# Latent queries and keys made feature-major, their rotary rows placed by transfers, and compressed attention taken into the middle of those products

## The chip, the cores and the metric

The kernel runs on one core of one Trainium2 chip. The metric is the device time of one execution in microseconds (us). The engines are named as in the profile: PE is TensorE (its matmuls), PEld its weight loads, DVE is VectorE, ACT is ScalarE, POOL is GpSimd, SP is SyncE, which here only issues transfers. Everything is in float32; a kernel before took 1770.38 us, the median of three runs (1769.51 to 1771.64).

## The reference

Two transformer blocks over 512 tokens and 1024 features: the first mixes native sparse attention (compressed, selected and windowed) with multi-head latent attention and ends in a gated convolutional feed-forward; the second has a Hyena and Fourier mixer and a mixture of 32 experts. The change touches the part of the first block between its input projection and its attention loop:

```python
proj = h @ w_in[i]
q_n, kv_n, gate_n, c_q, c_kv, k_r, merge = jnp.split(proj, offsets, axis=-1)
# compressed keys and values: 31 blocks of 32 tokens, stride 16
kb = (k[:, blk] + pos).reshape(B, n_cmp, G, CMP_BLOCK * dh)
k_cmp = jax.nn.gelu(kb @ w1 + b1) @ w2                      # and v_cmp alike
s_c = einsum('btgrd,bjgd->bgrtj', q, k_cmp) * scale - slopes * dist_c
p_cmp = _masked_softmax(s_c, dist_c >= 0);  o_cmp = p_cmp @ v_cmp
# latent attention: 8 heads, 64 plain + 32 rotary features in q and k, 64 in v
q  = (_rmsnorm(c_q, g_q) @ w_uq).reshape(B, T, H, QK_NOPE + QK_ROPE)
q_rope = _rope(q[..., QK_NOPE:], cos, sin)
kv = (_rmsnorm(c_kv, g_kv) @ w_ukv).reshape(B, T, H, QK_NOPE + V_DIM)
k_r = _rope(k_rope, cos, sin)                               # one set of rotary keys for all heads
s = (q_nope @ k_nope + q_rope @ k_r) * scale
```

## The kernel before, in words

Each engine has one hand-written program; semaphores order them. Weights come as 128x1024 tiles (`W[n]`) through a ring of 12 slots: SP waits until `w_used` says that tile n - 12 was used, then issues the load of tile n (L1469). PSUM is one array `pb` of eight banks of 128x512. A name such as `arena` in the profile is one large SBUF tensor which holds most of what is named below (`qTm`, `kTm`, `Vm`, `cqkv`, `chat`, `qkt`, `Pc`); `junk` is a separate 128x1024 scratch.

The stage in question starts when PE ends the products of the value columns and gates (L365, `split_columns`). After it PE does, in order:

1. the compression of keys and values, 256 small matmuls of 64x31 (L1661), ACT's GELUs (L1895, L1899), the second layer (L1669, L1670);
2. twelve transposes of the normed latents `chat` (L1677), copied by ACT into `cqT` (L1903);
3. four rounds, one for each 128 tokens: the up-projections of queries (L1691) and of keys and values (L1694), token-major; ACT copies the queries and DVE the keys and values into `qkt` (L1912, L2155 to L2157), DVE turns the rotary part (L2164 to L2169), PE transposes all 16 head tiles of queries and keys back to feature-major (L1705), and DVE and ACT copy them into `qTm` and `kTm` (L2172, L1916). `qkt` has two halves, but a round's transposes wait for its own copies, and the next round's products wait for the PSUM banks of this one;
4. compressed attention: scores of all heads against 31 blocks (L1716), a softmax of DVE and ACT over `Pc` (L2178 to L2202, ACT's exponential L1921), eight transposes (L1786), and the products with the compressed values (L1792). `scores(0)`, the first scores of the loop (L1740), stand before the transposes.

Then the attention loop runs: 48 units of two heads, in 12 groups `(i, kind)` of query tile and branch. Kind 2 is latent attention, its first unit is unit 16. `combine(w)` multiplies a finished group by its spread inverse sums; for the selected and windowed branches it writes into `junk` (L2240), first at unit 8. GpSimd (`h_back`, L1490) rebuilds `hT` from its two parts right after the value products; the DVE and ACT rounds wait for the end of it, because `qkt` overlays what it reads. After the loop come merge, output projection, feed-forward and the second block, whose last part, the experts, streams its weights.

SP sits in a loop over ring slots (L1469); the program raises `w_used` by 3 for the up-projection weights inside the compressed scores (L1716).

## Time and profile before

| | us |
|---|---|
| median of three runs (lowest, highest) | 1770.38 (1769.51, 1771.64) |
| the profiled execution, its own time | 1771.91 |
| its span from first to last instruction | 1770.1 |
| mean granted TensorE clock, 1 is 2.4 GHz | 0.939 |
| PE busy over the span | 1517.0 (86%) |
| DVE, ACT, POOL busy | 598.8, 477.2, 493.1 |

The profiled execution lasted 1.8 us longer than its span. Busy shares are means over stages with very different limits: the dense products of the first block, the attention loop, and the expert stream. For this change the table of the stretch from 95 to 180 us is what matters, since the work before and behind it is the same in both kernels. PEclk is the clock that was granted to TensorE: 1.00 is 2.4 GHz, 0.50 is 1.2 GHz.

### The profile page before, as it was taken

The numbers are of one execution on the slowest core, as the hardware profiler recorded it, in microseconds if no ns is written. First come the engines' busy times: TensorE is split into PE (matmuls) and PEld (weight loads), VectorE is DVE, ScalarE is ACT, GpSimd is POOL, SyncE is SP. The second block draws the span as 40 slices with busy tenths as digits, with TensorE's granted clock in tenths as the row PEclk, the third lists the DMA queues.
The fourth block names the chain that finished last, engine by engine and source line by source line (L and its number), as shares of the span: only waits on it lengthen the run. The fifth ranks groups of instructions, "written<-read, shape, count | busy, mean of one in ns | idle before, by whom it ended". The sixth has DMA issues, their size and how long they took to land.

```text
span 1770.1 us, 18813 instructions
## 1 busy us (share of the span) xinstructions
PE 1517.0 (86%) x7192; PEld 997.3 (56%) x7193; DVE 598.8 (34%) x1010; ACT 477.2 (27%) x818; POOL 493.1 (28%) x298
## 2 busy tenths in 40 slices
PE   7986999999979999999996999895877787877871
PEld 5964556788758888878774765474332232322320
DVE  3244565322263333322327685746100000000003
ACT  4232566322243333321325334221100000000001
POOL 3430113444334444444422362521101010000001
PEclk9986999999989999999997999996899999999996
DMA  7320000233223323323222221154699999999983
GB/s 277 103 84 36 1 1 2 84 95 96 83 83 96 95 96 95 96 89 92 93 84 89 84 71 60 48 209 183 274 426 427 427 428 425 426 422 425 425 343 150
DMA packets 47045, 315.25 MB, mean 178 GB/s; under 512 B 7344, under 2 KB 7344, under 8 KB 34560
## 3 DMA queue, kind: packets, MB, share of 16 engines
q1 hardware_dynamic: 37296, 286.80, 42.2%
q0 software_dynamic: 9104, 25.40, 3.9%
q10 hardware_dynamic: 576, 2.10, 0.3%
q8 instruction: 47, 0.77, 0.2%
q14 instruction: 22, 0.18, 0.0%
HBM read 307.98 MB, written 14.68 MB: 182 GB/s over the span
## 4 chain that ended last, share of the span: by engine, by line
PE 63%; DMA 19%; DVE 11%; issue 3%; ACT 2%; POOL 1%; SPq 0%; POOLq 0%; DVEq 0%; ACTq 0%
PE banks L355 23%; DMA arena<-experts 18%; PE banks L385 11%; PE banks L922 8%; PE banks L1821 2%; PE banks L365 2%; PE banks L1753 2%; PE banks L833 2%; PE banks L1769 1%; PE banks L690 1%; PE banks L1736 1%; PE banks L691 1%; PE banks L1740 1%; DVE arena_r L1611 1%; PE banks L1691 1%
## 5 line engine op out<-in xcount | busy, mean ns | idle before, releaser
L333 POOL TENSOR_TENSOR arena_r<-ring,arena_r 128x1024 fp32r<-128x1024 f32 x143 | 353.5, 2473 | 512.5 <-ACT arena_r L318 512.5
L355 PE MATMUL banks<-hT_r,arena_r 128*128 128x512 f32 x1216 | 397.0, 396 | 8.4 <-DVE arena_r L1611 5.7
L922 PE MATMUL banks<-ring,arena 128*64 128x512 f32 x768 | 245.4, 625 | 62.7 <-DMA arena<-experts 43.2
L355 PE MATMUL banks<-arena_r 128*128 128x512 f32 x800 | 295.8, 394 | 0.0
L318 ACT ACTIVATE arena_r<-ring 128x1024 fp32r<-128x1024 f32 x143 | 151.2, 1058 | 524.5 <-PE banks L355 325.0
L355 PEld LDWEIGHTS banks<-hT_r,arena_r 128*128 128x128 f32 x1216 | 228.4, 188 | 72.1 <-issue 8.9
L922 PEld LDWEIGHTS banks<-ring,arena 128*64 128x64 f32 x768 | 80.4, 144 | 215.5 <-issue 160.0
L385 PE MATMUL banks<-arena_r 128*128 128x512 f32 x784 | 187.9, 394 | 3.6 <-POOL arena_r L333 3.6
L355 PEld LDWEIGHTS banks<-arena_r 128*128 128x128 f32 x800 | 150.2, 188 | 35.0
L385 PEld LDWEIGHTS banks<-arena_r 128*128 128x128 f32 x784 | 147.2, 188 | 38.6 <-POOL arena_r L333 5.3
L589 POOL DMA_INDIRECT back<-arena,at_out x16 | 16.3, 1020 | 442.0 <-DVE arena L1386 228.9
L944 PE MATMUL banks<-arena 128*64 128x512 f32 x512 | 120.2, 624 | 21.3 <-DMA arena<-experts 15.8
L922 PE MATMUL banks<-arena 128*64 128x512 f32 x256 | 129.9, 666 | 0.0
L1381 DVE TENSOR_TENSOR arena<-arena,banks 128x512 f32<-128x512 f32 x16 | 11.0, 688 | 297.1 <-PE banks L922 297.1
L944 PEld LDWEIGHTS banks<-arena 128*64 128x64 f32 x512 | 40.9, 142 | 90.3 <-issue 78.7
L2320 DVE SCALAR_TENSOR_TENSOR arena<-banks,colt,arena 128x511 f32<-128x511 f32 x44 | 33.0, 749 | 157.5 <-ACT arena L2011 157.5
L1386 DVE COPY arena<-banks 128x512 f32<-128x512 f32 x16 | 11.1, 692 | 154.2 <-PE banks L944 154.2
L1589 PE MATMUL banks<-cst,arena 128*128 128x128 f32 x160 | 28.1, 349 | 39.0 <-DVE arena L1563 26.3
L1073 ACT ACTIVATE arena<-banks 128x512 f32<-128x512 f32 x16 | 9.6, 597 | 186.5 <-PE banks L930 186.5
L1934 ACT ACTIVATE arena<-banks,st 128x512 f32<-128x512 f32 (+3 forms) x96 | 49.9, 528 | 22.5 <-DVE st L2215 21.9
L344 DVE CAST arena_r<-arena 128x512 fp32r<-128x512 f32 x30 | 14.1, 471 | 111.7 <-PE banks L385 111.7
L1589 PEld LDWEIGHTS banks<-cst,arena 128*128 128x128 f32 x160 | 25.1, 184 | 42.5 <-issue 20.1
(404 smaller groups left out, 1882.8 us busy)
## 6 DMA issues: line engine op xcount, KB each, us to landing
arena<-experts SPq DMA_DIRECT2D x48, 2048.0 KB, 21.2
ring<-experts SPq DMA_DIRECT2D x48, 2048.0 KB, 18.2
ring<-stream SPq DMA_DIRECT2D x163, 512.0 KB, 3.5
rows<-arena POOLq DMA_DIRECT2D x8, 512.0 KB, 6.2
arena<-back POOLq DMA_DIRECT2D x8, 512.0 KB, 7.3
grow<-grows POOLq DMA_DIRECT2D x5, 512.0 KB, 4.6
resid<-x ACTq DMA_DIRECT2D x4, 512.0 KB, 5.5
out<-arena POOLq DMA_DIRECT2D x4, 512.0 KB, 3.0
```

The source lines that it names most:

```text
L318: nc.scalar.activation(parts(name, m)[:, 0, :], tile(tile_n), ACT.Copy).then_inc(S["w_high"], 1)
L333: nc.gpsimd.tensor_tensor(w[:, 1, :], tile(tile_n), plain(w[:, 0, :]), ALU.subtract).then_inc(S["w_low"], 1)
L355: last = nc.tensor.matmul(pb[:, bank, :], w[:, a, k * P:(k + 1) * P], b[:, k, :], start=(k == 0 and part == 0), stop=(k == ND - 1 and part ...
L365: last = nc.tensor.matmul(pb[:, bank0 + i, 0:width], a[:, k, i * P:(i + 1) * P], w[:, v, q * width:(q + 1) * width], start=(k == 0 and par ...
L385: last = nc.tensor.matmul(pb[:, 2 * i + h, :], u[row], w[:, v, h * 512:(h + 1) * 512], start=(k == 0 and part == 0), stop=(k == K - 1 and ...
L833: last = nc.tensor.matmul(pb[:, 2 * i + h, :], rows[row][:, i * P:(i + 1) * P], w[:, v, h * 512:(h + 1) * 512], start=(k == 0 and part == ...
L922: last = nc.tensor.matmul(pb[r, bank, :], XT[:, k, r], chunk(c + e)[:, k * 512:(k + 1) * 512], start=(k == 0), stop=(k == ND - 1))
L944: last = nc.tensor.matmul(pb[r, 3 + h, :], hbT[:, k, r], chunk(4 + e)[:, k * D + h * 512:k * D + (h + 1) * 512], start=(k == 0), stop=(k = ...
L1589: ins = nc.tensor.transpose(pb[:, bank0 + b, a * P:(a + 1) * P], src[:, a, b * P:(b + 1) * P], ident)
L1753: last = nc.tensor.transpose(pb[:, 4 + hh, kt * P:(kt + 1) * P], Pr[:, u % 2, hh, kt * P:(kt + 1) * P], ident)
L1821: last = nc.tensor.matmul(pb[:, b + w, :], tw[:, u, (4 * w + k) * P:(4 * w + k + 1) * P], src[:, k, :], start=(k == 0 and part == 0), stop ...
L1934: nc.scalar.activation(Pr[:, u % 2, hh, 0:nk], pb[:, 2 * (u % 2) + hh, 0:nk], ACT.Exp, scale=-1.0, bias=nm[:, u % 2, hh:hh + 1], accum_out ...
```

## The change

- The 64 transposes, and the token-major `qkt`, are gone. The weights are laid out anew on the host, so that the stationary operand is a weight block and the moving one is `cqT` with its 512 tokens: each product gives 128 features by 512 tokens, which is already the form of `qTm` and `kTm`. Two products hold the first and second rotary halves of the queries of all heads; four hold the plain query parts of heads j and j+4 (`q_nope`), four the plain keys of such pairs, and four, token-major still, the values.
- Cosine and sine, spread over the heads in `wide`, and the rotated keys (written back into `cqkv`) are transposed by PE (8 and 4 transposes), the first two scaled on the way (`cosT`, `sinT`). DVE multiplies both query halves with both (4 products of 128x512), GpSimd takes their difference and sum into `q_first` and `q_second`, the two halves of `junk`.
- Transfers within SBUF, issued by SP, put things in their places: one moves the plain queries of heads 4 to 7 from partitions 64 to 127 down to 0 to 63, one the keys likewise; 16 small ones place the rotary query rows by head; two copy the rotary keys for heads 5 to 7 and 0 to 3. SP issues them in its program order, behind the ring load of tile 33 and ahead of tile 34.
- The order on PE is new: transposes of the latents first, then compression, then the first three query products, the second layer of compression, a query product, the compressed scores, and behind them the ten remaining products, while DVE and ACT do the softmax of compressed attention. Its exponential stands on ACT behind three of the four copies of values.
- ACT's sine and square root come before its wait for the value products, and the gates are copied raw and put through the sigmoid later.
- New waits: each latent score waits for all 18 transfers (`qk_in`), and so does `combine(0)`; the first copies of turned probabilities wait for GpSimd's two (`q_rope`).

The diff, cut to what the prediction speaks of (the other hunks change PSUM bank numbers, semaphore names, the host's weight layout and 12 unused constant columns):

```diff
--- before.py
+++ after.py
...
-        qkt = ar(21216, 3072).rearrange("p (u w c) -> p u w c", u=2, w=2)
+        wide = ar3(23264, 2, 512)
+        cosT, sinT = ar(20192, 512), ar(20704, 512)
+        q_first, q_second = junk[:, 0:512], junk[:, 512:1024]
+        crossed = [ar(23264, 512), ar(23776, 512)]
...
-            with sp.Fori(1, W_EXP // RING) as turn:
+            def load(n):
+                sp.wait_ge(S["w_used"], n + 1 - RING)
+                sp.dma_start(ring[:, n % RING, :], W[n, :, :]).then_inc(landed[n % RING], 16)
+
+            def q_rows(h):
+                for part, src in enumerate((q_first, q_second)):
+                    at = DH + 16 * part
+                    sp.dma_start(qTm[at:at + 16, h, :], src[16 * h:16 * h + 16, :]).then_inc(S["qk_in"], 16)
+
+            def k_rows(a, b):
+                sp.dma_start(kTm[DH:QK, a:b, :], kTm[DH:QK, 4:5, :].broadcast_to([32, b - a, T])).then_inc(S["qk_in"], 16)
+
+            for n in range(RING, W_MERGE + RING):
+                load(n)
+
+            sp.wait_ge(S["mla_act"], 5)
+            sp.dma_start(qTm[0:DH, 4:8, :], qTm[DH:P, 0:4, :]).then_inc(S["shift_in"], 16)
+            k_rows(5, 8)
+            sp.wait_ge(S["q_rope"], 2)
+            for h in range(4, 8):
+                q_rows(h)
+            sp.wait_ge(S["shift_in"], 16)
+            for h in range(4):
+                q_rows(h)
+            sp.wait_ge(S["mla_act"], 11)
+            sp.wait_ge(S["mla_dve"], 11)
+            sp.dma_start(kTm[0:DH, 4:8, :], kTm[DH:P, 0:4, :]).then_inc(S["shift_in"], 16)
+            sp.wait_ge(S["shift_in"], 32)
+            k_rows(0, 4)
+            for n in range(W_MERGE + RING, 3 * RING):
+                load(n)
...
+            pool.wait_ge(S["mla_dve"], 9)
+            nc.gpsimd.tensor_tensor(q_first, q_first, crossed[0], ALU.subtract).then_inc(S["q_rope"], 1)
+            nc.gpsimd.tensor_tensor(q_second, q_second, crossed[1], ALU.add).then_inc(S["q_rope"], 1)
...
+            pe.wait_ge(S["mla_norm"], 1)
+            for b in range(3):
+                for i in range(NT):
+                    last = nc.tensor.transpose(pb[:, b, i * P:(i + 1) * P], chat[:, i, b * P:(b + 1) * P], ident)
+                last.then_inc(S["mla_tr"], 1)
+
+            pe.wait_ge(S["proj_v_ev"], 2)
+            for b, bank in ((0, 3), (1, 6)):
+                pe.wait_ge(S["mla_dve"], b + 1)
+                for i in range(NT):
+                    last = nc.tensor.transpose(pb[:, bank, i * P:(i + 1) * P], wide[:, b, i * P:(i + 1) * P], ident)
+                last.then_inc(S["mla_tr"], 1)
+            pe.wait_ge(S["mla_dve"], 3)
+            for i in range(NT):
+                last = nc.tensor.transpose(pb[0:QK, 7, i * P:(i + 1) * P], cqkv[:, i, 320:416], ident)
+            last.then_inc(S["mla_tr"], 1)
+
             pe.wait_ge(S["cmp_blocks"], 4)
-            pe.wait_ge(S["proj_mla_ev"], NT)
...
+            for n in (W_UQ, W_UQ + 1, W_UKV):
+                arrived(pe, n)
+
+            def q_up(at, bank):
+                for k in range(2):
+                    last = nc.tensor.matmul(pb[:, bank, :], tile(W_UQ + k)[:, at:at + P], cqT[:, k, :], start=(k == 0), stop=(k == 1))
+                return last
+
+            def q_nope(j, bank):
+                q_up(256 + j * P, bank).then_inc(S["mla_up"], 1)
+
+            pe.wait_ge(S["mla_tr_ev"], 3)
+            q_up(0, 0)
+            q_up(P, 1).then_inc(S["mla_up"], 1)
+            q_nope(0, 2)
...
             pe.wait_ge(S["cmp_gelu"], 5)
+            pe.wait_ge(S["mla_dve"], 5)
...
+            q_nope(1, 3)
...
+            q_nope(2, 4)
+            pe.wait_ge(S["mla_dve"], 9)
+            q_nope(3, 0)
+
+            for i, bank in enumerate((7, 1, 2, 3)):
+                pe.wait_ge(S["mla_act"], (1, 1, 2, 3)[i])
+                nc.tensor.matmul(pb[:, bank, :], cqT[:, 2, i * P:(i + 1) * P], tile(W_UKV)[:, 512:1024], start=True, stop=True)\
+                    .then_inc(S["mla_up"], 1)
+            for j, bank in enumerate((6, 5, 4, 7)):
+                if j == 0:
+                    pe.wait_ge(S["cs_dve"], 1)
+                if j >= 2:
+                    pe.wait_ge(S["mla_act"], (4, 6)[j - 2])
+                last = nc.tensor.matmul(pb[:, bank, :], tile(W_UKV)[:, j * P:(j + 1) * P], cqT[:, 2, :], start=True, stop=True)
+                last.then_inc(*((S["mla_up"], 1) if j < 3 else (used, 3)))
...
+            pe.wait_ge(S["mla_act"], 7)
...
+            nc.scalar.activation(gates[:, :, :], pb[:, 4:8, 256:280], ACT.Copy).then_inc(S["proj_v_ev"], 1)
+            nc.scalar.activation(Vsw[:, :, :], pb[:, 4:8, 0:256], ACT.Copy).then_inc(S["proj_v_ev"], 1)
+            for b in range(3):
+                act.wait_ge(S["mla_tr"], b + 1)
+                nc.scalar.activation(cqT[:, b, :], pb[:, b, :], ACT.Copy,
+                                     scale=col("g_q", b) if b < 2 else col("g_kv")).then_inc(S["mla_tr_ev"], 1)
+            act.wait_ge(S["proj_v_ev"], 1)
+            nc.scalar.activation(gates[:, :, :], gates[:, :, :], ACT.Sigmoid).then_inc(S["proj_v_ev"], 1)
...
+            act.wait_ge(S["mla_tr"], 6)
+            nc.scalar.activation(kTm[DH:QK, 4, :], pb[DH:QK, 7, :], ACT.Copy).then_inc(S["mla_act"], 1)
+            for j, bank in enumerate((2, 3, 4, 0)):
+                act.wait_ge(S["mla_up"], 2 + j)
+                nc.scalar.activation(qTm[:, j, :], pb[:, bank, :], ACT.Copy, scale=QK_SCALE).then_inc(S["mla_act"], 1)
+
+            def v_up(i):
+                act.wait_ge(S["mla_up"], 6 + i)
+                nc.scalar.activation(Vm[:, i, :], pb[:, (7, 1, 2, 3)[i], :], ACT.Copy).then_inc(S["mla_act"], 1)
+
+            for i in range(3):
+                v_up(i)
             act.wait_ge(S["cs_dve"], 2)
             nc.scalar.activation(Pc[:, :, :, 0:31], Pc[:, :, :, 0:31], ACT.Exp).then_inc(S["cs_act"], 1)
+            v_up(3)
+            for j, bank in enumerate((6, 5)):
+                act.wait_ge(S["mla_up"], 10 + j)
+                nc.scalar.activation(kTm[:, j, :], pb[:, bank, :], ACT.Copy).then_inc(S["mla_act"], 1)
...
+            for b, t in enumerate((cos, sin)):
+                nc.vector.tensor_copy(wide[:, b, :].rearrange("p (i h f) -> p i h f", i=NT, h=HEADS),
+                                      by_tile(t).unsqueeze(2).broadcast_to([P, NT, HEADS, 16])).then_inc(S["mla_dve"], 1)
...
+            nc.vector.tensor_tensor(by_tile(r1), x1, by_tile(cos), ALU.mult)
+            nc.vector.tensor_tensor(by_tile(r2), x2, by_tile(sin), ALU.mult)
+            nc.vector.tensor_tensor(by_tile(r3), x2, by_tile(cos), ALU.mult)
+            L(nc.vector.tensor_tensor(by_tile(r4), x1, by_tile(sin), ALU.mult))
+            nc.vector.tensor_tensor(x1, by_tile(r1), by_tile(r2), ALU.subtract)
+            nc.vector.tensor_tensor(x2, by_tile(r3), by_tile(r4), ALU.add).then_inc(S["mla_dve"], 1)
+
+            for b, (dst, bank) in enumerate(((cosT, 3), (sinT, 6))):
+                dve.wait_ge(S["mla_tr"], 4 + b)
+                nc.vector.tensor_scalar(dst, pb[:, bank, :], QK_SCALE, None, ALU.mult).then_inc(S["mla_dve"], 1)
+
+            dve.wait_ge(S["mla_up"], 1)
+            dve.wait_ge(S["mla_dve"], 5)
+            for dst, bank, t in ((q_first, 0, cosT), (crossed[1], 0, sinT), (q_second, 1, cosT), (crossed[0], 1, sinT)):
+                nc.vector.tensor_tensor(dst, pb[:, bank, :], t, ALU.mult).then_inc(S["mla_dve"], 1)
...
+                    if w == 0:
+                        dve.wait_ge(S["qk_in"], 16 * 18)
...
+            dve.wait_ge(S["h_back"], ND)
+            for j, bank in ((2, 4), (3, 7)):
+                dve.wait_ge(*((S["mla_up"], 12) if j == 2 else (S["w_used"], W_MERGE)))
+                nc.vector.tensor_copy(kTm[:, j, :], pb[:, bank, :]).then_inc(S["mla_dve"], 1)
```

In both kernels a float32 matmul is one row here and two instructions in the trace. PE behind the value products, before (`cst` is the identity of a transpose, `ring` a weight tile, 64x31 the compression):

```order
L365 MATMUL banks<-arena_r 128x280
L1661 MATMUL banks<-arena,ring 64x31 [waits w_landed3,proj_mla_ev,cmp_blocks]
L1661 MATMUL banks<-arena,ring 64x31 x31
...
L1669 MATMUL banks<-arena,colt 64x31 [waits cmp_gelu]
L1670 MATMUL banks<-colt,arena 128x64
...
L1677 MATMUL banks<-cst,arena 128x128 [waits mla_norm,proj_v_ev]
L1677 MATMUL banks<-cst,arena 128x128 x11
```

and in the changed kernel:

```order
L1693 MATMUL banks<-cst,arena 128x128 [waits mla_norm]
L1693 MATMUL banks<-cst,arena 128x128 x11
L1700 MATMUL banks<-cst,arena 128x128 [waits mla_dve,proj_v_ev]
...
L1704 MATMUL banks<-cst,arena 96x128 [waits mla_dve]
L1704 MATMUL banks<-cst,arena 96x128 x3
L1714 MATMUL banks<-arena,ring 64x31 [waits w_landed3,cmp_blocks]
L1714 MATMUL banks<-arena,ring 64x31 x31
```

The transposes of the latents moved ahead of compression, and 12 more joined them; compression now waits for nothing of the latents but stands behind them.

PE from the second layer of compression on, before (96x128 are transposes of head tiles, 128x31 the compressed scores that follow later):

```order
L1677 MATMUL banks<-cst,arena 128x128 [waits mla_norm,proj_v_ev]
L1677 MATMUL banks<-cst,arena 128x128 x11
L1691 MATMUL banks<-ring,arena 128x384 [waits w_landed8,w_landed7,w_landed9,cmp_ready,mla_tr_ev]
L1691 MATMUL banks<-ring,arena 128x384 x3
L1694 MATMUL banks<-ring,arena 128x512 x2
L1705 MATMUL banks<-cst,arena 96x128 [waits kv_ev,q_ev]
L1705 MATMUL banks<-cst,arena 96x128 x15
L1691 MATMUL banks<-ring,arena 128x384 [waits kv_ev,q_ev]
```

and in the changed kernel (128x512 with `ring` are the up-projections, 128x31 the compressed scores):

```order
L1724 MATMUL banks<-arena,ring 128x512 [waits w_landed9,mla_tr_ev,w_landed8,w_landed7]
L1724 MATMUL banks<-arena,ring 128x512 x5
L1739 MATMUL banks<-arena,colt 64x31 [waits mla_dve,cmp_gelu]
L1740 MATMUL banks<-colt,arena 128x64
L1739 MATMUL banks<-arena,colt 64x31
L1740 MATMUL banks<-colt,arena 128x64
L1724 MATMUL banks<-arena,ring 128x512 x2
L1750 MATMUL banks<-arena 128x31 [waits cmp_ready]
L1750 MATMUL banks<-arena 128x31 x31
L1724 MATMUL banks<-arena,ring 128x512 x2
L1724 MATMUL banks<-arena,ring 128x512 [waits mla_dve]
L1724 MATMUL banks<-arena,ring 128x512
```

The rounds of product and transposes became one row of products, with the compressed scores after the fifth group of them; nothing that waits for a copy of a whole round is left.

ACT behind the GELUs in the changed kernel (32x512 the rotary keys, then four query copies, value copies, the exponential, key copies); before, four rounds of one 128x768 and two 96x4x128 copies stood there, and the exponential behind them all:

```order
L1960 ACTIVATE arena<-banks 32x512 [waits mla_tr,h_back]
L1963 ACTIVATE arena<-banks 128x512 [waits mla_up] x4
L1967 ACTIVATE arena<-banks 128x512 [waits mla_up] x3
L1972 ACT_TABLE_LOAD
L1972 ACTIVATE arena<-arena 128x32x31 [waits cs_dve]
L1967 ACTIVATE arena<-banks 128x512 [waits mla_up]
L1976 ACTIVATE arena<-banks 128x512 [waits mla_up] x2
L1979 ACTIVATE arena<-banks 128x512 [waits cs_pe] x2
```

The exponential of compressed attention now stands between the third and the fourth copy of values, so it can't begin before the third value product.

SP in the changed kernel from the ring loads on (64x2048 the moves of heads 4 to 7, 16x512 the rotary query rows, 32x3x512 and 32x4x512 the rotary keys):

```order
L1470 DMA ring<-stream 128x1024 [waits w_used] x22
L1484 DMA arena<-arena 64x2048 [waits mla_act]
L1478 DMA arena<-arena 32x3x512
L1475 DMA arena<-junk 16x512 [waits q_rope]
L1475 DMA arena<-junk 16x512 x7
L1475 DMA arena<-junk 16x512 [waits shift_in]
L1475 DMA arena<-junk 16x512 x7
L1494 DMA arena<-arena 64x2048 [waits mla_dve,mla_act]
L1478 DMA arena<-arena 32x4x512 [waits shift_in]
L1470 DMA ring<-stream 128x1024 [waits w_used] x2
```

All 20 transfers stand behind the last of the 22 ring loads, which waits for the last up-projection; before there was nothing between the ring loads.

## Rows read from the trace of the kernel before

**Rows 1.** Windows: stretch, length, busy us of PE, PEld, DVE, ACT, POOL; clock, DMA share, GB/s.
```profile
95.00:180.00 85.00, 61.02 (x482) 40.90 (x481) 36.02 (x78) 24.11 (x38) 11.86 (x10) 0.74 0.16 50
```
**Rows 2.** The chain that ended last, 109 to 180 us: start, length, what.
```profile
109.56 5.10 PE banks L1691 x8
...
124.00 1.73 PE banks L1694 x4
125.97 0.68 DVE arena L2156
...
171.08 1.98 PE banks L1786 x8
...
179.99 0.42 PE banks L1740 x4
```
**Rows 3.** Groups of instructions, 90 to 185 us: busy, mean ns, idle before.
```profile
L1705 PE MATMUL banks<-cst,arena 128*96 128x128 f32 x64 | 12.2, 368 | 11.8 <-DVE arena L2169 11.8
...
L1661 PE MATMUL banks<-arena,ring 64*64 64x31 f32 x256 | 7.8, 218 | 0.2 <-issue 0.2
...
L1716 PE MATMUL banks<-arena 64*128 64x31 f32 x64 | 4.6, 304 | 0.7 <-ACT arena L1916 0.7
```
**Rows 4.** Timeline of DVE, ACT and POOL, 90 to 107 us: start, length, instruction.
```profile
90.72 0.15 DVE L2113 TENSOR_SCALAR st<-st 128x4 f32<-128x4 f32 x1
94.98 1.02 ACT L1886 ACTIVATE arena<-banks 128x1024 f32<-128x1024 f32 x1 [6.66 <-PE banks L365]
95.02 11.26 POOL L1490 TENSOR_TENSOR hT<-hT_r,arena_r 128x512 f32<-128x512 f32 x8 [4.24 <-PE banks L365]
99.21 1.28 ACT L1892 ACT_TABLE_LOAD   x1
100.98 1.29 DVE L2116 TENSOR_TENSOR arena<-arena,st 128x1024 f32<-128x1024 f32 x1
103.86 1.28 DVE L2129 TENSOR_TENSOR arena<-arena 128x64 f32<-128x64 f32 x1
106.40 0.22 DVE L2131 TENSOR_TENSOR arena<-arena 128x64 f32<-128x64 f32 x1
```
**Rows 5.** Timeline of PE: three kinds of float32 products at half clock.
```profile
105.02 0.68 PE L1670 MATMUL banks<-colt,arena 64*128 64x64 f32 x2
105.63 2.82 PE L1677 MATMUL banks<-cst,arena 128*128 128x128 f32 x12
173.73 6.26 PE L1792 MATMUL banks<-arena 128*64 128x512 f32 x16 [0.69 <-ACT arena L1924]
```
**Rows 6.** Windows of 2 us; columns as in rows 1.
```profile
104.00:106.00 2.00, 2.00 (x10) 1.64 (x9) 1.97 (x2) 0.00 (x0) 2.00 (x2) 0.50 0.68 256
114.00:116.00 2.00, 2.00 (x6) 0.76 (x4) 0.00 (x0) 0.00 (x0) 0.00 (x0) 0.96 0.00 0
124.00:126.00 2.00, 1.72 (x5) 0.41 (x3) 0.24 (x2) 0.24 (x1) 0.00 (x0) 1.00 0.00 0
160.00:162.00 2.00, 0.41 (x4) 0.27 (x4) 1.21 (x2) 0.00 (x0) 0.00 (x0) 0.50 1.03 420
```
**Rows 7.** Timeline: steps of the softmax, and copies.
```profile
107.61 1.84 DVE L2140 COPY arena<-banks 32x64 f32<-32x64 f32 x8
116.48 0.29 DVE L2155 COPY arena<-arena 128x256 f32<-128x256 f32 x1 [7.03 <-PE banks L1694]
161.71 1.26 DVE L2181 TENSOR_TENSOR arena<-banks,arena 128x496 f32<-128x496 f32 x2
166.67 1.03 ACT L1921 ACTIVATE arena<-arena 128x992 f32<-128x992 f32 x1 [9.61 <-DVE arena L2191]
199.13 0.69 DVE L2240 TENSOR_TENSOR junk<-banks,arena 128x512 f32<-128x512 f32 x1 [1.03 <-ACT arena L1949]
```
**Rows 8.** SP's three ring loads at 157 us: shortest, median, longest issue in ns, and landing.
```profile
L1469 SPq DMA_DIRECT2D ring<-stream x3: 332/333/1453, 157.1 to 158.3; - x3
...
DMA to landing us min/median/max: 4.6/5.3/5.9
```

148 lines of the change are left out of this document (34 added, 114 removed).

## The prediction, made before the changed kernel had run

> **What bounds the kernel now.** I read the page first, then windows, the chain, the groups by line and the timeline of the stretch from 95 to 180 us. The change touches only this stretch; what stands before and behind it is the same work in the same order. There PE is busy 61.0 of 85.0 us, at a mean clock of 0.74, and DVE, ACT and POOL are each busy under half of it [rows 1]: no engine is full, so the stage is a chain of hand-overs. The chain shows them: products at 109.56, then in the second round products until 125.7, DVE from 125.97, and so on until the loop starts at 179.99 [rows 2]. The transposes of the four rounds hold PE for 12.2 us and it stands 11.8 us before them, waiting for DVE [rows 3]. Then the compressed scores (4.6 us) and a softmax beside which PE does nearly nothing: the first addition at 161.71, the exponential at 166.67, the transposes at 171.08, then 6.26 us of products at half clock [rows 2, 5, 7].
>
> **The stretch anew, step by step.** I rebuild it from 94.9 us, the end of the value products, to the first unit of the loop, and take the difference to the 180.0 of now. Moments are estimates from the rows' durations, with 0.25 us from PE to a reader and 0.05 between others, my own allowance.
>
> *Prices.* A float32 product of 128x512 over 128 rows is two instructions; four take 1.73 us on the chain at 124.00 [rows 2], where the clock is 1.00 [rows 6]: 0.43 each, 0.86 a product, double at half clock. A transpose is 2.82/12 = 0.23 at half clock [rows 5], about 0.11 at full. A copy or product of DVE or ACT out of PSUM with 512 columns is 0.69 [rows 7].
>
> *Norm and rotary tables.* ACT's sine and root now come in the 6.66 us in which it waited for the value products [rows 4], each behind a table load of 1.28. The row sums are ready at 90.87 [rows 4]. DVE then does two new spread copies (0.29 for 256 columns [rows 7], so 0.56 each), 0.2, 1.29 and half of 1.29: the normed latents are there at about 94.1, before PE wants them. So the norm, now awaited from 100.98 on, is off the path.
>
> *Transposes ahead of compression.* 12 + 8 + 4 of them, 24 x 0.11 = 2.6 us. The last four want the rotated keys, six small steps of DVE. Four fit before 95.0; the last two fall beside POOL's eight additions, where a step of 64 columns took 1.28 against 0.22 after they ended [rows 4]. So keys at 97.8, compression from 98.1: 3.2 us later than now. (Without that contention 97.5, so the price has both ends within 0.6.)
>
> *Compression*: 7.8 us [rows 3] at full clock. Now the clock reads 0.50 from 104 on [rows 6], some 9 us after the dense products ended. I let it fall at the same moment: compression ends at 107.9, 2.0 us of that from the clock.
>
> *First three query products*: 6 x 0.86 = 5.2 us. Now the clock is back to 0.96 in 114 to 116 [rows 6], 4.5 us after dense products began at 109.56. The same here gives half clock to 112.4 and adds 2.2: 115.3. ACT's GELUs (1.1 us after compression) lie beside them.
>
> *Second layer and ready*: four small products, 1.0 us (two took 0.68 at half clock [rows 5]): 116.3. Then DVE's nine copies, 0.2 + 1.84 [rows 7], and a hand-over at each end: 118.7. One query group (two products, 1.7) lies beside them. DVE's four products with the tables (2.8 us) start at 114 and end just as these copies may start. POOL's two additions (11.26/8 = 1.4 us each [rows 4]) now fall beside the nine copies, which read PSUM; no row shows such a pair. Nothing is one end; if both block the copies, as they do a step within SBUF, 2.8 us is the other. I take nothing, since PSUM steps don't look like those of L2129, and keep 2.8 for the range.
>
> The Trainium skill, "SBUF — State Buffer", section "SBUF: two separate sides", says that GpSimd shuts out a DVE step only where that has two SBUF inputs or runs in a two-port mode. [...]
>
> *Compressed scores*: 4.6 us for 64 instructions now, of which the last part ran at half clock, since 160 to 162 reads 0.50 [rows 3, 6]. I take 4.2: 123.0. This was at 160.4.
>
> *The other products*: two query groups (four products), four of values, four of keys, 12 x 0.86 = 10.3, and 1.5 for a clock that falls in the small scores once more and comes back at 126: 134.8. In all there are 20 such products for 24 of before with as many columns (20 x 512 = 16 x 384 + 8 x 512), so nothing is saved in them. Saved are 64 transposes and the hand-overs around them.
>
> *The softmax beside them.* From the first addition to the exponential it is 161.71 to 166.67 [rows 7], 5.0 us, so DVE's part is done at 128.3. But the exponential stands behind three value copies on ACT: the third value product ends after 7 x 0.86 + 1.5, at 130.5, its copy at 131.4, the table load (1.28 [rows 4]) at 132.7, the exponential (1.03 [rows 7]) at 133.7. From its end to the transposes DVE now takes 167.70 to 171.08 [rows 2, 7], 3.4 us: 137.1. Here ACT's order ends last, and DVE has 3 us to spare.
>
> *Transposes and products with compressed values*: 8 x 0.11, ACT's second copy 0.7, 3.3 us for what took 6.26 at half clock [rows 5], hand-overs 0.5: the loop starts at 142.5 if the clock is full, as dense products ran until 134.8.
>
> So 180.0 - 142.5 = 37.5 us earlier.
>
> **What could give it back in the loop.** The 20 transfers stand on SP behind the load of tile 33, which waits for the last key product, 134.8. Three ring loads go first and land 4.6 to 5.9 us after their issue [rows 8]. Of the transfers no row of this kernel shows the like (within SBUF, half the partitions, 512 KB for the two largest). Lower bound: the issues alone, 20 x 0.33 = 7 us [rows 8]. Upper: four steps that wait for one another (ring loads, query move, key move, key rows), 5.9 us each, and the issues: 134.8 + 23.6 + 7 = 165. I take 5.3 for the loads and 4 for each later step, half the issues hidden: 154. The first who waits is `combine(0)`, now at 199.13, 19.1 us after the loop starts [rows 7]: at 161.6. So there are 7 us of cover by my value, and 4 us are lost at the upper bound. The first latent score is unit 16, later still. POOL's two additions end by 120, and who waits for them starts behind 140.
>
> Trainium skill, "SBUF — State Buffer", section "Door 1: The DMA port swizzle": partitions 0 to 63 reach only half of the ports, so a 64-row transfer gets no more bandwidth than a 32-row one, 196 GB/s for 1 MiB. By that page the two moves of 512 KB are an estimated 2.7 us of transfer more than a fixed 2 us each, which would leave the sum as it is; no row shows it yet.
>
> **Sum.** The profiled execution took 1771.91; less 37.5 gives 1734.4. The median of three lies 1.5 below that execution, so the forecast for the median is **1733**.
>
> **Rivals.**
> 1. *The clock stays halved.* For: the compression and the compressed scores are small products, and the stretch now runs at 0.74, at 0.50 in its softmax [rows 1, 6]. Against: dense products brought it back within 5 us. If it is 0.50 from 104 to the end of the stage, the rebuild gives compressed scores at 130.6, keys at 150.9, loop at 162.5: 17.5 saved, 1753. If it halves only from the compressed scores on, 154.5, and 1745.
> 2. *The transfers come late*, at the upper bound or somewhat beyond: 4 to 12 us lost, 1737 to 1745. For: 18 of them on one semaphore, and each step waits for the one before. Against: 27 us between the last product and the wait.
> 3. *Full clock throughout*: small products keep the clock up when they stand in a dense stream. Then the loop starts at 136: 1727. Against: PE was busy all of 104 to 106, with 0.50 [rows 6]. The Trainium skill, "TensorE: Matmul & The Clock Gate", section "What's actually happening", says that a busy array releases the throttle and idleness brings it back; by that the clock would hold here, as in this rival.
> 4. *Slower than before.* One mechanism: the transfers within SBUF run on one of the 16 engines each instead of on all. 420 GB/s [rows 6] is 26 GB/s per engine. Two moves of 512 KB are then 20 us each, 448 KB of rotary keys 17, 16 rows of 32 KB another 20: 77 us behind 140 ends at 217, and `combine(0)`, which needs them at 161.6, waits 55. That is 18 us slower, 1788. It decides from 59 us of transfers on: 21.6 of cover behind 140, and the 37.5 gained. Against: the ring loads, of the same kind of issue, use all engines.
> 5. *The change does not do what it says*, for instance something outside the rebuilt stretch holds the loop, and the time stays within 0.2%: nothing in the chain speaks for it.
>
> **Chances.** Forecast (1729 to 1741) 0.63; rival 1 0.14; rival 2 0.09; rival 3 0.08; rival 4 0.04; rival 5 0.02. All but the last two are faster. What a measurement of this kernel can tell from no change is about 0.2%, 3.5 us. Faster 0.94, same 0.02, slower 0.04. The range is 1726 to 1752: it holds the forecast, rivals 2 and 3 and most of rival 1.
>
> **What will show it.** In the changed trace: compression (now L1714) starting at 98 and not 95; PE's products in one run with the compressed scores at 119 to 123; the exponential waiting for the copy of values (its predecessor on ACT) and not for DVE; compressed values' transposes at 137; the first score of unit 1 at 142; the granted clock 1.00 from 126 on. `combine(0)` should wait for ACT's spread inverse as now and for no DMA. The forecast is wrong if the clock reads 0.50 behind 126, if DVE idles before L2204 or PE before the compressed scores by more than 2 us, or if the span from loop start to the end is not what it is now, 1590 us.

## The result, and the profile after

| | before | after |
|---|---|---|
| median, us (lowest, highest) | 1770.44 (1769.51, 1771.64) | 1727.51 (1726.66, 1730.80) |
| profiled execution; its span | 1771.91; 1770.1 | 1730.80; 1729.0 |
| mean granted clock | 0.939 | 0.948 |
| PE busy; DVE, ACT, POOL busy | 1517.0; 598.8, 477.2, 493.1 | 1497.3; 586.5, 475.4, 494.1 |

The ratio is 0.9761 (95% interval 0.9744 to 0.9778): 42.9 us faster. Forecast were 1733, with a range of 1726 to 1752. The measured time lies in the range, but 1.5 us below the forecast's own band of 1729 to 1741, which had a chance of 0.63.

The windows of the rebuilt stretch in the changed kernel, from the end of the value products to the first score of the loop, and four windows of 2 us in it (columns as in rows 1):

```profile
94.09:137.12 43.03, 41.16 (x427) 25.21 (x426) 18.10 (x34) 19.02 (x34) 12.93 (x12) 0.96 0.34 108
114.00:116.00 2.00, 2.00 (x40) 2.00 (x40) 0.33 (x1) 0.00 (x0) 0.00 (x0) 1.00 0.04 8
116.00:118.00 2.00, 2.00 (x20) 1.45 (x19) 0.93 (x2) 0.00 (x0) 0.00 (x0) 0.75 0.00 0
118.00:120.00 2.00, 2.00 (x4) 0.85 (x3) 1.93 (x3) 0.00 (x0) 0.00 (x0) 0.50 0.00 0
120.00:122.00 2.00, 2.00 (x5) 0.76 (x4) 1.97 (x2) 0.60 (x1) 0.00 (x0) 0.90 0.00 0
```

Read it against [rows 1]: 43.0 us for 85.0. PE stood idle for 24.0 us then (85.00 - 61.02) and for 1.9 now (43.03 - 41.16), 22.1 less; and it was busy 19.9 us less, at a clock of 0.96 for 0.74. The last four rows show the one place where the clock still falls, in the compressed scores.

The chain that ended last, in the changed kernel (start, length, what; L1693 transposes of the latents, L1714 compression, L1724 queries, L1750 compressed scores, L1759 values, L1834 turned probabilities, L1842 products with compressed values):

```profile
94.25 1.31 PE banks L1693 x12
...
97.04 7.58 PE banks L1714 x256
104.62 5.35 PE banks L1724 x12
...
113.20 3.76 PE banks L1750 x64
116.96 5.33 PE banks L1724 x8
122.28 2.59 PE banks L1759 x6
124.89 0.60 ACT arena L1967
...
126.81 1.04 ACT arena L1972
127.87 1.20 DVE st L2229
...
131.22 0.67 PE banks L1834 x4
...
133.05 3.65 PE banks L1842 x16
...
137.12 1.02 PE banks L1800 x8
```

Where [rows 2] change engine in every round, this is PE's own work from 94 to 125, with one stretch of DVE (the copies at 111.2 to 113.2, beside a query group), then one passage through ACT and DVE. The loop starts at 137.12; [rows 2] had it at 179.99. That is 42.9 us earlier: 42.2 of them lie in the stretch (from the end of the value products, 94.94 before and 94.25 now, it is 85.05 us before and 42.87 now), and 0.7 lie ahead of it, in work that the change doesn't touch.

The timeline of the changed kernel, the instructions that the prediction named (L2192 the last step of the rotated keys, L2207 the copies answering to L2140 of [rows 7], L1527 the first of two additions, the second follows at 112.08, L2278 `combine(0)`):

```profile
93.62 0.22 DVE L2192 TENSOR_TENSOR arena<-arena 128x64 f32<-128x64 f32 x1
94.33 9.85 POOL L1524 TENSOR_TENSOR hT<-hT_r,arena_r 128x512 f32<-128x512 f32 x8 [4.20 <-PE banks L368]
110.86 1.26 POOL L1527 TENSOR_TENSOR junk<-junk,arena 128x512 f32<-128x512 f32 x1 [6.67 <-DVE arena L2201]
111.30 1.84 DVE L2207 COPY arena<-banks 32x64 f32<-32x64 f32 x8
...
127.87 1.19 DVE L2229 TENSOR_REDUCE st<-arena 128x32 f32<-128x992 f32 x1 [5.87 <-ACT arena L1972]
155.82 0.69 DVE L2278 TENSOR_TENSOR junk<-banks,arena 128x512 f32<-128x512 f32 x1 [1.01 <-issue]
```

DVE has done its part of the softmax at 122.0 (127.87 - 5.87) and then waits for ACT's exponential. `combine(0)` comes 18.7 us after the loop's start (19.1 before [rows 7]) and waits for no DMA.

SP's issues in the changed kernel (start, length of the group; L1484 and L1494 the moves of 512 KB, L1478 the rotary keys, L1475 the 16 query rows):

```profile
130.50 0.57 SPq L1484 DMA_DIRECT2D arena<-arena  x1
...
131.88 13.78 SPq L1475 DMA_DIRECT2D arena<-junk  x16
145.77 0.52 SPq L1494 DMA_DIRECT2D arena<-arena  x1
149.95 0.64 SPq L1478 DMA_DIRECT2D arena<-arena  x1
```

and the page's list of DMA issues for 100 to 200 us (name, count, KB each, median us to landing):

```profile
arena<-arena SPq DMA_DIRECT2D x2, 512.0 KB, 6.8
arena<-junk SPq DMA_DIRECT2D x16, 32.0 KB, 3.2
...
arena<-arena SPq DMA_DIRECT2D x1, 256.0 KB, 3.2
```

The last transfer lands at 149.95 + 3.2 = 153.2, 2.6 us before `combine(0)`. The 16 rows took 13.78 us to issue, 0.86 each. The two moves of 512 KB landed after 9.5 us (queries, behind three ring loads) and 4.2 us (keys).

### The profile page after: what moved, and what is told of

The parts are those of the page before. It is cut to its first block, busy times and chain, and to the rows that moved or that the text cites. A ratio compares the mean times of both kernels' runs of the same rounds, so it can differ in the third digit from the quotient of the medians.

```text
span 1729.0 us, 18608 instructions
## 1 busy us (share of the span) xinstructions
PE 1497.3 (87%) x7132; PEld 983.7 (57%) x7133; DVE 586.5 (34%) x976; ACT 475.4 (27%) x818; POOL 494.1 (29%) x300
## 4 chain that ended last, share of the span: by engine, by line
PE 64%; DMA 19%; DVE 10%; issue 3%; ACT 2%; POOL 1%; SPq 0%; POOLq 0%; ACTq 0%; DVEq 0%
PE banks L358 24%; DMA arena<-experts 18%; PE banks L388 11%; PE banks L925 9%; PE banks L1871 3%; PE banks L368 2%; PE banks L1800 2%; PE banks L836 2%; PE banks L1816 1%; PE banks L693 1%; PE banks L1783 1%; PE banks L694 1%; PE banks L1787 1%; DVE arena_r L1648 1%; PE banks L1626 1%
## 5 line engine op out<-in xcount | busy, mean ns | idle before, releaser
L388 PEld LDWEIGHTS banks<-arena_r 128*128 128x128 f32 x784 | 147.0, 188 | 39.5 <-POOL arena_r L336 5.3
L1626 PE MATMUL banks<-cst,arena 128*128 128x128 f32 x160 | 28.4, 353 | 39.5 <-DVE arena L1600 27.0
L347 DVE CAST arena_r<-arena 128x512 fp32r<-128x512 f32 x30 | 14.2, 472 | 112.1 <-PE banks L388 112.1
```

The costliest lines, as they stand in the source:

```text
L388: last = nc.tensor.matmul(pb[:, 2 * i + h, :], u[row], w[:, v, h * 512:(h + 1) * 512], start=(k == 0 and part == 0), stop=(k == K - 1 and ...
L1626: ins = nc.tensor.transpose(pb[:, bank0 + b, a * P:(a + 1) * P], src[:, a, b * P:(b + 1) * P], ident)
```

## The experiments

All are edits of the changed kernel, but for one of the kernel before. Ratios are to the kernel before, with 95% intervals; differences are of medians, and medians of the changed kernel itself, timed twice, differed by 0.9 us. A difference between two edits of under about 2 us is therefore read from the traces too, or called open. In comparisons a moment is counted from the end of the value products, since that wanders by a microsecond from profile to profile of the changed kernel and its edits (93.3 to 94.7).

**Compressed scores last.** They stand behind all products, and the softmax with them.

```diff
-            (64 compressed scores, behind q_nope(1, 3))
...
+            pe.wait_ge(S["mla_act"], 11)
+            (64 compressed scores, behind the key products)
```

> The changed kernel with its compressed scores moved behind all up-projections, and the exponential behind all value and key copies; everything else is kept. My theory: of the 43 us gained, a part comes from laying the softmax beside the ten remaining products. Without that, PE ends the products about 3.8 us earlier (at 124.8), does the scores until about 129.5 after ACT's last key copy, and then stands through DVE's 5.0 us, the exponential 1.0 and DVE's 3.4; transposes at about 139.5 instead of 131.2, and a falling clock adds up to 4 us in the products with compressed values: loop at 145 to 149 instead of 137.1, time 1736 to 1740. Rival: the softmax was never the last thing, only the feature-major form counts; then within 2 us of 1727.5.

Measured: 1735.81 us (1734.46 to 1736.93), ratio 0.9808 (0.9793 to 0.9823). PE's timeline at the turned probabilities in that kernel:

```profile
135.98 1.97 PE L1833 MATMUL banks<-cst,arena 128*128 128x128 f32 x8 [8.55 <-DVE arena L2234]
```

and two windows in the softmax:

```profile
126.00:128.00 2.00, 1.43 (x14) 0.60 (x12) 1.35 (x3) 0.00 (x0) 0.00 (x0) 1.00 0.95 238
...
134.00:136.00 2.00, 0.02 (x1) 0.02 (x1) 1.90 (x5) 0.00 (x0) 0.00 (x0) 0.50 0.29 66
```

PE waits 8.55 us for the softmax, in which the clock goes from 1.00 to 0.50, and the eight transposes behind it take 1.97 us for 1.09 in the version with all three edits (below). Taking the scores to the middle is worth 8.3 us, a fifth of the gain; by subtraction the other 34.6 come with the form and order of the products. From the end of the value products to the loop it is 51.2 us here for 42.9 in the changed kernel, the same 8.3.

**The norm early, alone**, in the kernel before: ACT's sine and square root ahead of its wait for the value products.

```diff
+            act.wait_ge(S["ang_ready"], 1)
+            nc.scalar.activation(ropet[:, 0:128], ropet[:, 128:256], ACT.Sin).then_inc(S["sin_ready"], 1)
+            act.wait_ge(S["mla_ms"], 1)
+            nc.scalar.activation(mrt, mss, ACT.Sqrt).then_inc(S["mla_rt"], 1)
             act.wait_ge(S["w_used"], W_CMP)
```

> The kernel before with one part of the change alone: ACT's sine and square root ahead of its wait for the value products. My theory: the norm was not on the path there, since PE does the compression (until 102.9) and its second layer first; the transposes could start about 0.0 to 0.5 us earlier, and DVE's small steps leave POOL's additions: 1769.5 to 1770.5. Rival: the norm and the rotary steps held up the copies that end cmp_ready, then 1 to 3 us are gained.

Measured: 1770.42 us (1769.26 to 1774.47), ratio 1.0003 (0.9993 to 1.0012). Nothing: in the old order compression and the second layer stand ahead of the latents' transposes, which start at 105.63 without a wait [rows 5]. The norm was not what ended last.

**The transposes' work, and their hand-overs.** Two kernels put 64 transposes back that nobody reads: the first in one run, the second in four lots that each wait for a copy.

```diff
+            pe.wait_ge(S["mla_act"], 1)
+            for n in range(64):
+                nc.tensor.transpose(pb[0:QK, 7, (n % 4) * P:(n % 4 + 1) * P], cqT[:, 2, 0:QK], ident)
             for i, bank in enumerate((7, 1, 2, 3)):
```
```diff
                     .then_inc(S["mla_up"], 1)
+                pe.wait_ge(S["mla_act"], 6 + i)
+                for n in range(16):
+                    nc.tensor.transpose(pb[0:QK, bank, (n % 4) * P:(n % 4 + 1) * P], cqT[:, 2, 0:QK], ident)
```

> The changed kernel, with 64 transposes of 96x128 added on TensorE in one run ahead of the first value product; they read the ready latents, write a bank that the product then overwrites, and nobody waits for them. It prices the work of the 64 transposes that the change took out, without their hand-overs. Theory A (work only): 64 x 0.13 us (what twelve took in the changed kernel, 1.5 us) = 8.3 us, all on the path, since the softmax's first part ends at 122 and the exponential stands behind the third value product: 1735.8 (1734.5 to 1737). Theory B (the clock is the real price of transposes: in the kernel before they took 12.2 us for 64): the granted clock falls to 0.50 within the run, 12 us for them and 3 or more for the products behind: 1742 or more. Theory C: they cost under 4 us, since the softmax covers them: 1731 or less.

> The same 64 transposes, but 16 behind each of the four value products, each lot waiting until ScalarE has copied that product, as the lots of the kernel before waited for their copies. The difference to the kernel with all 64 in one run is the price of four hand-overs in their shortest form (product, copy, transposes). Theory A: each hand-over leaves TensorE idle for one copy, 0.6 us, and 0.25 us on either side, 1.1 us; the fourth copy stands behind the exponential, table load and all, 1.3 + 1.0 us more: 3 x 1.1 + 3.5 = 6.8 us over the other kernel, 1742 to 1744. Rival: the waits also bring the clock down to 0.50, as in the kernel before: then another 5 us or more, 1747 or above.

Measured: 1734.63 us (1733.20 to 1736.94), ratio 0.9799 (0.9782 to 0.9815); and 1737.35 us (1736.45 to 1737.92), 0.9812 (0.9796 to 0.9828). The chain of the first has all 64 on it; in the chain of the second each lot has a hand-over of 0.02 + 0.61 + 0.04 us ahead of it. The chain of the first:

```profile
122.58 6.99 PE banks L1759 x64
```

and the second:

```profile
126.28 0.02 issue
126.31 0.61 ACT arena L1970
126.91 0.04 issue
126.96 1.95 PE banks L1763 x16
```

The work costs 7.1 us (7.0 on the chain, 0.109 each), four hand-overs in their shortest form 2.7 (4 x 0.67). I had set 0.13 for a transpose, from a group's busy time, and 6.8 us for the hand-overs: both too high, since the copy starts 0.02 us behind the product and the exponential fits between two lots. The clock read 1.00 in both from the first of these transposes to the last. So of the 42.9 us the transposes' work and their shortest hand-overs are 9.8. The kernel before lost more by the length of its waits (four rounds in which PE idled 3.0 us each, 11.8 in all [rows 3], where the shortest form costs 0.67), by the softmax, and by the clock. A token-major kernel with its rounds interleaved, which would keep the transposes and shorten the waits, was not run.

**The second layer early**: straight behind compression, where PE must wait for the GELUs.

```diff
+            (second layer, with its waits for cmp_gelu and mla_dve)
             pe.wait_ge(S["mla_tr_ev"], 3)
             q_up(0, 0)
```

> The changed kernel with the second layer of compression placed right behind the first, as in the kernel before, so that PE waits for ACT's GELUs and does small products before the first query products. Theory A, on the clock: it stayed at full because dense products followed the compression at once; with the wait of about 1 us and 1.2 us of small products it falls to 0.50 at about 105 as before, for some 4 us: 1.1 for the wait and 2 for the clock less about 1 for a compressed softmax that may start earlier, time 1729 to 1731. Theory B: the clock does not depend on this, only on what went before compression; then the clock stays at 1.00 until 117 and the time is 1727.5 to 1729.

Measured: 1731.77 us (1731.25 to 1735.70), ratio 0.9789 (0.9774 to 0.9804), 4.3 slower. PE's timeline in that kernel:

```profile
105.96 0.27 PE L1734 MATMUL banks<-arena,colt 64*64 64x31 f32 x2 [1.12 <-ACT arena L1955]
...
107.11 5.40 PE L1724 MATMUL banks<-arena,ring 128*128 128x512 f32 x8
```

and two windows:

```profile
106.00:108.00 2.00, 2.00 (x10) 1.39 (x11) 0.00 (x0) 0.32 (x1) 0.00 (x0) 0.96 0.88 277
108.00:110.00 2.00, 2.00 (x3) 0.67 (x2) 0.00 (x0) 0.00 (x0) 0.00 (x0) 0.50 0.23 92
```

A gap of 1.12 us and four small products, and the clock falls in the dense products behind them. In the kernel before it falls behind a wait for the same GELUs too, of 0.91 us, and there already in the small products (the 0.50 of [rows 6]):

```profile
103.80 0.33 PE L1669 MATMUL banks<-arena,colt 64*64 64x31 f32 x2 [0.91 <-ACT arena L1899]
```

By the profiles the loop starts 3.5 us later (46.4 for 42.9 from the end of the value products): 1.1 is the wait, 2.0 the clock (5.40 us for eight products, at 0.43 each 3.44), 0.4 the rest; PE waits another 1.00 us for DVE's copies ahead of the scores. The 0.8 up to the 4.3 of the medians isn't in these profiles. In the changed kernel dense products stand behind the compression, and the clock stays at 1.00. This run moves the gap and the four small products together, so it doesn't show which of them counts. A gap alone isn't enough: in the kernel before PE idled from 116.4 to 119.5, and the clock still read 1.00, as it did until 126:

```profile
116.00:118.00 2.00, 0.38 (x1) 0.00 (x0) 1.50 (x4) 0.81 (x1) 0.00 (x0) 1.00 0.00 0
118.00:120.00 2.00, 0.53 (x5) 0.54 (x6) 1.38 (x7) 0.00 (x0) 0.00 (x0) 1.00 0.00 0
```

**A query group between the compressed scores.**

```diff
                         last = nc.tensor.matmul(pb[:, 6 - g, at:at + 31], ...)
+                if i == 1:
+                    q_nope(2, 4)
             last.then_inc(S["cs_pe"], 1)
-            q_nope(2, 4)
```

> The changed kernel with one query group (two products, 1.7 us) moved from behind the compressed scores into their middle. My theory: the only half clock left in the stage, from 117 to 120.6, comes from 3.8 us of small scores in one piece; if dense products between them keep the clock at 1.00, PE ends its products 1.8 us earlier, while the softmax starts 1.7 us later but has 3.5 us to spare before the exponential: the transposes start at 131.2 as ACT allows, or 1 us sooner, 1726.5 to 1727.5. Rival: the clock falls anyway, and the later softmax costs nothing or up to 1.7 us: 1727.5 to 1729.

Measured: 1726.21 us (1725.52 to 1726.79), ratio 0.9754 (0.9737 to 0.9770). Its windows:

```profile
116.00:118.00 2.00, 2.00 (x33) 1.86 (x32) 0.00 (x0) 0.60 (x1) 0.00 (x0) 1.00 0.00 0
118.00:120.00 2.00, 2.00 (x7) 1.01 (x6) 1.74 (x3) 0.00 (x0) 0.00 (x0) 1.00 0.00 0
```

The same instructions in another order, and 0.75 and 0.50 have become 1.00: the last fall of the clock is gone. All nine profiles of kernels with these scores in one piece between dense products (the changed kernel twice and seven edits) show the fall, and neither of the two with a group between them does. The fall had cost 1.9 us in the changed kernel's profile (5.33 us for eight products, at 0.43 each 3.44). The median is 1.3 us lower, but the slowest execution, 1726.79, lies above the fastest of the changed kernel, 1726.58; by the traces the loop starts 1.4 us sooner (41.5 for 42.9).

**The exponential first**, ahead of the three value copies; then with it **the turned probabilities ahead of `scores(0)`**.

```diff
-            for i in range(3):
-                v_up(i)
             act.wait_ge(S["cs_dve"], 2)
             nc.scalar.activation(Pc[:, :, :, 0:31], ...)
+            for i in range(3):
+                v_up(i)
```
```diff
-            pe.wait_ge(S["mla_act"], 7)
-            scores(0)
             pe.wait_ge(S["cs_dve"], 3)
...
+            scores(0)
             pe.wait_ge(S["cs_act"], 3)
```

> The changed kernel with one move on ACT: the exponential of compressed attention ahead of the copies of values. My theory: ACT's order delays the softmax; the exponential then ends at about 125.2 instead of 127.9 and the softmax at 128.6 instead of 131.2, but PE is in its products until 129.1 and in the first scores until 130.2, so the transposes start at 130.2 and the loop 1.0 us earlier: 1726.5. Rival: the late value copies hold back PE's last key product or the first scores (bank 7, banks 0 and 1), and the time stays or grows by 1 us.

> As the kernel with the exponential first, and on PE the eight transposes of compressed attention stand ahead of the first scores of the loop. My theory: transposes at 129.1, ACT's two copies beside the first scores, products with compressed values from about 131.6 instead of 133.05, loop at about 135.7 instead of 137.1: 1.4 us less than the changed kernel, 1726.1. Rival: the first scores come later, and DVE's maxima and ACT's exponentials of unit 0 end after the products with compressed values, which gives the gain back: 1727.5.

Measured: 1727.92 us (1726.52 to 1728.55), ratio 0.9759 (0.9744 to 0.9774); and 1725.32 us (1723.49 to 1726.04), 0.9746 (0.9733 to 0.9759). The first was a miss: 1726.5 was expected. PE had no wait left in it between the scores and the turned probabilities, but in its profile the clock fell earlier:

```profile
114.00:116.00 2.00, 2.00 (x33) 2.00 (x32) 0.00 (x0) 0.00 (x0) 0.00 (x0) 0.77 0.00 0
...
120.00:122.00 2.00, 2.00 (x4) 0.69 (x3) 1.84 (x2) 0.60 (x1) 0.00 (x0) 0.52 0.00 0
```

The edit need not be the cause. The second profile of the changed kernel itself (the last run below) shows the same, a line of its windows and one of its chain:

```profile
120.00:122.00 2.00, 2.00 (x3) 0.67 (x2) 1.83 (x2) 0.60 (x1) 0.00 (x0) 0.50 0.00 0
```
```profile
116.82 6.60 PE banks L1724 x8
```

Scores and the eight products behind them take 10.7 us in it, as in the kernel with the exponential first, for 9.1 in the first profile: two executions of one kernel differ by 1.6 us in one fall of the clock, and why they do stays open. Beside the execution with an equally long fall the edit does start the loop 1.1 us sooner (43.4 for 44.5 us from the end of the value products), as was expected; the medians don't show it. In the second kernel neither ACT nor DVE stands in the chain between the key products and `scores(0)` (0.87 of transposes, then 1.06 of `scores(0)`). It is 2.2 us faster than the changed kernel, and its five executions all lie below the nine of that kernel.

**The query moves ahead of three ring loads**, and **each row transfer twice** (the copy goes to a buffer in memory, and all waits count it).

```diff
-            for n in range(RING, W_MERGE + RING):
+            for n in range(RING, W_UQ + RING):
                 load(n)
...
+            for n in range(W_UQ + RING, W_MERGE + RING):
+                load(n)
             sp.wait_ge(S["mla_act"], 11)
```
```diff
+                    to = 32 * h + 16 * part
+                    sp.dma_start(rows[to:to + 16, 0:512], src[16 * h:16 * h + 16, :]).then_inc(S["qk_in"], 16)
```

> The changed kernel with SP's three ring loads of tiles 31 to 33 moved behind the query transfers, which then start as soon as ACT has copied the plain queries (123) instead of behind the last key product (130.5). My theory: the transfers are hidden by the loop's first 18.7 us, with 2.6 us to spare; so they end some 6 us earlier and the time does not move: within 1 us of 1727.5. Rival: combine(0) already waits for them in part, then 1 to 3 us are gained.

> The changed kernel with a second copy of each of the 16 rotary row transfers, to a place in memory that nobody reads then; the waits count all 34. My theory: SP needs 0.86 us for each of these transfers (13.8 us for 16), and the last one lands at 153.2, only 2.6 us before combine(0) at 155.8. Sixteen more take 13.8 us more, so combine(0) waits about 11 us, the loop's end moves by most of it: 1736 to 1739. Rival: the issues overlap or the wait has other slack (DVE's lateness is taken up by two buffers of each kind), and the time stays within 2 us of 1727.5.

Measured: 1727.63 us (1726.61 to 1728.52), ratio 0.9760 (0.9744 to 0.9777), no change: the transfers cost nothing where they stand. The first issue comes about 7.5 us sooner, counted from the end of the value products, but the last only about 3.7. The query move, with no ring load ahead of it, landed after 4.3 us (9.5 in the changed kernel), and the key move, now behind the three, after 8.6 (4.2):

```profile
137.89 0.51 SPq L1496 DMA_DIRECT2D arena<-arena  x1
146.47 0.64 SPq L1478 DMA_DIRECT2D arena<-arena  x1
```

Twice as many: 1736.38 us (1733.70 to 1738.42), 0.9816 (0.9799 to 0.9832), 8.9 slower. DVE's timeline at `combine(0)` in that kernel:

```profile
161.91 0.69 DVE L2280 TENSOR_TENSOR junk<-banks,arena 128x512 f32<-128x512 f32 x1 [7.31 <-DMA arena<-arena]
```

and SP's:

```profile
158.61 0.64 SPq L1480 DMA_DIRECT2D arena<-arena  x1
```

158.61 and a landing of 3.2 us give 161.8. The cover is real and thin: the last issue came 8.7 us later (158.61 for 149.95), `combine(0)` 6.1 later. The wait is 7.3 us where about 11 were expected, since the 32 rows followed one another at 0.67 us and not at 0.86. How much of the wait reaches the end isn't settled: the medians differ by 8.9 us, but the two profiled executions, the slowest of the one kernel and the fastest of the other, by 2.9.

**All three**: split scores, exponential and turned probabilities first, and all 20 transfers ahead of the ring loads of tiles 31 to 35. Beside it **the changed kernel again**.

> The changed kernel with the compressed scores split by a query group, the exponential first on ACT, the transposes of compressed attention ahead of the first scores, and all transfers ahead of the ring loads of tiles 31 to 35. My theory: the clock stays full and PE ends its products 33.5 us after the value products; the softmax, whose scores end 1.9 us later than in the unsplit order, is ready at 34.3 and is now the last; products with compressed values from 36.4 instead of 38.8 us, loop 2.4 us earlier than in the changed kernel, 1725.1 or a little less, and combine(0), which comes sooner, is not held because the transfers end earlier too. Rival: the gains of the two orders add up (1.4 and 2.0 us), 1724.0. Second rival: the wait for the softmax takes both back, 1726 to 1727.

> The changed kernel itself, unaltered, beside the one with the three orders on the same chip: 1727 to 1728, so that a difference of 2 us can be read.

Measured: 1724.61 us (1723.49 to 1725.08), ratio 0.9745 (0.9732 to 0.9758), and 1728.38 us (1726.58 to 1729.16), 0.9764 (0.9750 to 0.9777): 3.8 us better than the changed kernel on the same chip, with no execution in common. It can't be told from the version with the exponential and the turned probabilities first (ratio 0.9746), whose executions overlap its own. Its window from the end of the value products to the loop:

```profile
94.11:134.49 40.38, 39.54 (x426) 24.45 (x424) 18.19 (x34) 18.58 (x34) 12.94 (x12) 1.00 0.36 96
```

and its chain:

```profile
118.97 1.26 DVE arena L2215 x2
...
127.09 1.20 DVE arena L2236
...
128.34 1.09 PE banks L1833 x8
```

Clock 1.00 throughout and PE busy 39.5 of 40.4 us: what is left is work. The split makes the scores end about 2 us of work later, so the softmax, not PE's products, is now what the turned probabilities wait for last. The loop starts 2.5 us sooner than in the changed kernel's first profile (40.4 for 42.9), which the theory had at 2.4.

## Why the prediction was right

The gain is there where it was looked for, and the mechanism (a chain of hand-overs and a halved clock become one row of products) held. By PE's rows the gain in the stretch splits so, as an estimate: 22.1 us of idle time gone; 5.7 of work, 52 transposes fewer at 0.109; the remaining 14.2 of busy time is work done at full clock that was done at half. Busy time multiplied by the granted clock, added up over pieces of 0.5 us, gives nearly the same: 44.5 us of work at full clock before and 39.5 now, so 5.0 of work and 14.8 of clock. The size was less well forecast: the time missed the band of the forecast and came out where rival 3 had put it.

The forecast was 5.4 us short in what is saved, 4.7 of them in the stretch; the other 0.7 are the earlier end of the value products. Its steps, counted from the end of the value products (94.9 in the prediction, 94.25 on the chain):

- *Ahead of compression*: 3.2 forecast, 2.8 measured. The last key step ended at 93.84, before GpSimd began at 94.33, so the contention that was priced at 0.6 did not occur. That the norm is "off the path" now was true, but it had not been on it before.
- *Compression, 9.8 forecast, 7.6 measured*, and *first query groups, 7.4 forecast, 5.35 measured*. **These are the mis-sized terms: the 2.0 and the 2.2 us for a clock that falls at 104.** I had read the fall in [rows 6] as something that small products bring, a while after dense ones end. The early second layer shows what I had left out: in the old order a wait of about 1 us and four small products stood between the compression and the dense products. The row of 104 to 106, busy throughout at 0.50, which I held against rival 3, comes right behind that wait. The new order has neither there, and the clock is 1.00 up to 116. The Trainium skill, "TensorE: Matmul & The Clock Gate", section "What's actually happening", says that a busy array releases the throttle and idleness brings it back. By that rule both terms would have been dropped, and the trace agrees here.
- *Second layer, copies, ready*: 3.4 forecast, 3.2 measured. The nine copies took 1.84 us beside POOL's additions, to the hundredth what L2140 took [rows 7]. So the open price is 0, as I took it, and not 2.8. The Trainium skill, "SBUF — State Buffer", section "SBUF: two separate sides", has GpSimd shut out DVE only where DVE has two SBUF inputs or a two-port mode; the trace agrees for copies out of PSUM.
- *Compressed scores*: 4.3 and 3.8. *Products to the third of values*: 7.5 and 7.9, of which the fall of the clock was forecast at 1.5 and took 1.9. Here the rule of the Trainium skill cited above does not suffice: PE is busy 2.00 of 2.00 us in every row, and the clock falls; with a query group between the scores it does not. It was right to keep this term.
- *Softmax*: as told, DVE is early and the exponential stands behind three copies. From the third value copy to the turned probabilities it is 6.3 us (124.89 to 131.22), forecast 6.6 (130.5 to 137.1).
- *To the loop*: 5.4 forecast, 5.9 measured.

That sums to 47.6 forecast and 42.9 measured. The time of rival 3, full clock throughout, 1727, is the one that came, though not its whole condition: one fall stayed. It had a chance of 0.08. Its loop start of 136 is 41.1 us from the end of the value products; the version with all three edits, at full clock throughout, has 40.4. Rival 1 was refuted, rivals 4 and 5 too.

*Transfers.* The sum of the prediction has a slip: 134.8, 5.3 for the loads, three steps of 4 and half of 7 us of issues are 155.6 and not 154. The end was forecast at 154 and the start of `combine(0)` at 161.6; measured 153.2 and 155.8. The price of an issue was wrong: 0.33 us is a load of 128 rows [rows 8], while the 16-row transfers took 0.59 to issue (median) and followed each other at 0.86. That was made good by an earlier start (130.5) and a last landing of 3.2 us. But the cover was 2.6 us and not 7: the 5 us by which the loop came earlier are taken from it. I had held the cover fixed by the forecast start, though what covers is the time from loop start to `combine(0)`, 18.7 us. Rival 2 was nearer than its 0.09 suggests: 16 more transfers brought it about. The Trainium skill, "SBUF — State Buffer", gives 196 GB/s at 1 MiB for 64 rows (section "Door 1: The DMA port swizzle") and a fixed 2 us for a transfer (section "The DMA setup-cost knee"), from which I estimate 2.7 + 2 us for a move of 512 KB. The key move was there for the next issue after 4.18 us (145.77 to 149.95), which is near it, and far from the 20 us of rival 4. The estimate is near for a move with nothing waiting ahead of it on SP's queue: behind three ring loads the query move took 9.5 us, where the prediction had 4 for a step.

The span from loop start to the end was given as 1590: 1591.9 in the changed profile (1729.0 - 137.12), 1.8 more, in an execution that lay 3.3 above its median. In the profiles of the edits, but for the one whose `combine(0)` waits for transfers, it is 1586 to 1590, so nothing is seen to be given back later.

## What to carry to other kernels

A stage of product, copy, transpose, copy can cost more by its waits and by the clock that falls among them than by its transposes (here 22 us idle and some 14 of clock, for the 7 us that 64 transposes take): lay out weights so that the product comes in the form that its reader wants, and lay what is left, a softmax, beside the run of dense products. Ask of each fall of the clock in the old profile what stands ahead of it, a gap or a run of small products, and whether that survives the change. Keep dense products between groups of small ones, and count the cover of a transfer from the event that moves with the change, here the loop's start.
